# The down projection of a ConvFFN, by seven products of quarters instead of one full product

## The reference, cut to what matters

```
up   = rms_norm(x, g_pre_ffn) @ w_up                # 1024 -> 2 * 2816
conv = b_conv + sum(w_conv[i] * buf[:, i:i + t])    # width 3, causal
hid  = gelu(gate) * val                             # 2816 features
ff   = hid @ w_down                                 # 2816 -> 1024
x    = x + rms_norm(ff, g_post_ffn)
```

## Time and profile before

| | us |
|---|---|
| runs, median (lowest to highest) | 2139.41 (2137.74 to 2140.78) |
| the profiled execution's own time | 2138.59 |
| its span | 2136.8 |
| granted clock of TensorE, mean | 0.994 |
| the 18 Strassen stages, period of each | 21.6 |
| first and last matmul of the down half | 1848.9 and 2127.4 |
| busy in the span: PE, DVE, ACT, POOL | 2070.1, 1419.5, 958.1, 742.8 |

### The profile page before, as it was taken

The page is one execution under the profiler, slowest core; times in us unless marked ns, Lnnn a source line. Parts: engine busy times, 40 slices in busy tenths (PEclk is TensorE's granted clock), DMA queues, the critical chain, the costliest instruction groups (busy, mean ns, idle before and its releaser), DMA issues. The chain is left out here.

```text
span 2136.8 us, 35593 instructions
## 1 busy us (share of the span) xinstructions
PE 2070.1 (97%) x13704; PEld 1953.3 (91%) x13704; DVE 1419.5 (66%) x2242; ACT 958.1 (45%) x1773; POOL 742.8 (35%) x499
## 2 busy tenths in 40 slices
PE   5999999998999999999999999999999999999998
PEld 5998999998899999998999978899999999988875
DVE  5956544443787788857556557598888888834565
ACT  4334534433777777754342122243333333423343
POOL 2333355554644454436565210003333334100000
PEclk9999999999999999999999999999999999999999
DMA  5434344768546555546666433311222222563654
GB/s 175 116 98 133 131 166 166 206 187 238 150 120 144 125 131 142 136 149 176 190 183 205 157 126 99 89 61 61 72 74 79 67 86 62 194 206 127 217 183 163
DMA packets 313278, 298.65 MB, mean 140 GB/s; under 512 B 51767, under 2 KB 275991, under 8 KB 313111
## 3 DMA queue, kind: packets, MB, share of 16 engines
q1 hardware_dynamic: 299776, 265.61, 42.8%
q10 hardware_dynamic: 11094, 22.65, 2.9%
q0 software_dynamic: 2240, 8.13, 1.0%
HBM read 210.03 MB, written 86.30 MB: 139 GB/s over the span
## 5 line engine op out<-in xcount | busy, mean ns | idle before, releaser
L1786 DVE TENSOR_TENSOR_SCAN p_rest<-p_rest 128x896 f32<-128x896 f32 (+7 forms) x128 | 215.0, 1692 | 78.4 <-ACT p_rest L1705 78.4
L1555 POOL TENSOR_TENSOR p_weights<-p_weights,p_rest 128x895 f32<-128x895 f32 (+7 forms) x128 | 162.4, 1275 | 202.6 <-DVE p_rest L1786 202.6
L3355 DVE TENSOR_TENSOR p_w_lo<-p_w_raw,p_w_hi 128x512 fp32r<-128x512 f32 (+1 forms) x168 | 161.0, 963 | 54.4 <-ACT p_w_hi L3147 54.3
L3147 ACT ACTIVATE p_w_hi<-p_w_raw 128x512 fp32r<-128x512 f32 (+1 forms) x186 | 139.3, 772 | 68.0 <-DVE p_rows L3374 37.0
L172 PE MATMUL p_psB<-hT_lo,w_hi 128*128 128x274 f32 (+2 forms) x528 | 161.4, 306 | 4.2 <-issue 2.4
L174 PE MATMUL p_psB<-hT_hi,w_lo 128*128 128x274 f32 (+2 forms) x528 | 159.2, 302 | 0.0
L173 PE MATMUL p_psB<-hT_hi,w_hi 128*128 128x274 f32 (+2 forms) x528 | 159.1, 301 | 0.0
L172 PE MATMUL ps_up<-mergedT_lo,p_w_hi 128*128 128x274 f32 (+1 forms) x488 | 149.2, 306 | 4.1 <-DVE p_rows L3438 1.7
L1130 DVE TENSOR_TENSOR p_x<-p_psB,p_x 128x274 f32<-128x274 f32 (+1 forms) x168 | 70.6, 436 | 118.8 <-PE p_psB L174 113.0
L174 PE MATMUL ps_up<-mergedT_hi,p_w_lo 128*128 128x274 f32 (+1 forms) x488 | 148.4, 304 | 0.0
L173 PE MATMUL ps_up<-mergedT_hi,p_w_hi 128*128 128x274 f32 (+1 forms) x488 | 148.3, 304 | 0.0
(11 more groups left out here) (456 smaller groups left out, 7053.1 us busy)
## 6 DMA issues: line engine op xcount, KB each, us to landing
p_w_raw<-in_w_down SPq DMA_DIRECT2D x66, 512.0 KB, 3.8
p_w_raw<-in_w_up SPq DMA_DIRECT2D x44, 512.0 KB, 5.1
hid_scratch<-p_rows ACTq DMA_DIRECT2D x22, 545.0 KB, 2.9
p_raw_more<-in_w_in SPq DMA_DIRECT2D x20, 512.0 KB, 5.2
w_raw<-in_w_in SPq DMA_DIRECT2D x20, 512.0 KB, 5.3
p_kT<-k_hi_scratch SPq DMA_DIRECT2D x32, 256.0 KB, 4.7
p_kT<-k_lo_scratch SPq DMA_DIRECT2D x32, 256.0 KB, 5.2
w_raw<-in_w_gate SPq DMA_DIRECT2D x16, 512.0 KB, 5.0
```

Of the source, the lines that this page charges most:

```text
L1555: nc.gpsimd.tensor_tensor(wt[:, b % 6, 0:n - 1], wt[:, b % 6, 0:n - 1], rest[:, b % 4, 1:n], ALU.mult).then_inc(s("weights"), 1)
L1786: nc.vector.tensor_tensor_scan(src, src, src, 1.0, ALU.mult, ALU.bypass).then_inc(s("scanned"), 1)
L3147: nc.scalar.activation(target(w_hi, key), source(key), ACT.Copy).then_inc(s("w_hi"), 1)
L3355: nc.vector.tensor_tensor(target(w_lo, key), source(key), target(w_hi, key).bitcast(F32), ALU.subtract).then_inc(s("built"), 1)
```

## The change

The down product gets Strassen's scheme too. The contraction halves are the even and the odd f (11 pairs p, `FP`), the token halves are the lower and upper 512 prompt tokens, the column halves are columns 0 to 511 and 512 to 1023. `DOWN` names the seven products in their order, P1, P2, P5, P6, P3, P7, P4, each over 11 pairs: 77 passes, each of four token tiles with 512 columns, 12 matmuls (924 in all). The 64 sample rows are not part of the scheme: they are multiplied plainly beside P1 and P2 (left half) and P3 and P7 (right half), three matmuls in each of 44 passes (132), as the first of a pass.

The operands are sums: of hidden rows (four sums for each pair, made by POOL during the up half and kept in DRAM in `hid_sums_scratch`) and of quarters of `w_down` (four for each pair, made by POOL in the down half, T1 to T4). The stages in which POOL works on hidden sums are those of `SUMS_OF`: pairs 0 to 2 at f = 6, 7, 8, pairs 3 to 8 at f = 10, 12, 14, 16, 18, 20; pairs 9 and 10 after the last stage. At the start of such a stage POOL issues two loads, at its end it does four additions of 128x512 and issues a store of 1 MB. The products are combined on DVE as they leave PSUM, partly on POOL.

```diff
+    FP = FT // 2
+    DOWN = ("P1", "P2", "P5", "P6", "P3", "P7", "P4")
+    PASSES = [(j, p) for j in range(len(DOWN)) for p in range(FP)]
+    DOWN_BANKS = (4, 5, 6, 7, 1, 2, 3)
+    SUM_AT = {"P6": 0, "P7": 1, "P3": 2, "P5": 3}
+    SUMS_OF = {**{6 + p: p for p in range(3)}, **{2 * p + 4: p for p in range(3, FP - 2)}}
-    BY_TILE = 3
+    BY_TILE = 4
...
@block.gpsimd
+                def bring_hid(p):
+                    pool.wait_ge(s("hid_stored"), 16 * (2 * p + 2))
+                    if p:
+                        pool.wait_ge(s("sums_stored"), 16 * p)
+                    else:
+                        pool.wait_ge(s("t_lo"), 8)
+                    for f in (2 * p, 2 * p + 1):
+                        pool.dma_start(sums[:, 2 * (f % 2):2 * (f % 2) + 2, :].rearrange("p a c -> p (a c)"),
+                                       d.hid[f][:, GAP:GAP + SEQ]).then_inc(s("sums_ready"), 16)
+                def sum_hid(p):
+                    pool.wait_ge(s("sums_ready"), 32 * (p + 1))
+                    for n, (dst, left, right, op) in enumerate(((3, 1, 3, ALU.add), (1, 1, 0, ALU.subtract), (0, 3, 0, ALU.subtract),
+                                                                (2, 2, 0, ALU.subtract))):
+                        if n > 1:
+                            pool.wait_ge(s("hid_sums"), 4 * p + n)
+                        nc.gpsimd.tensor_tensor(sums[:, dst, :], sums[:, left, :], sums[:, right, :], op).then_inc(s("hid_sums"), 1)
+                    pool.wait_ge(s("hid_sums"), 4 * p + 4)
+                    pool.dma_start(d.hs[p], sums[:]).then_inc(s("sums_stored"), 16)
                 for f in range(PLAIN, FT):
                     n, b = 4 * fast(f), 2 * f
+                    if f in SUMS_OF:
+                        bring_hid(SUMS_OF[f])
                     ... (L3016 to L3026)
+                    if f in SUMS_OF:
+                        sum_hid(SUMS_OF[f])
+                for p in (FP - 2, FP - 1):
+                    bring_hid(p)
+                    sum_hid(p)
+                for p in range(FP):
+                    b_sum("T1", p)
+                for p in range(FP):
+                    b_sum("T2", p)
...             (u4 for 4 tiles, T3 for all p, T4 for p < 4, scale_row for 4 tiles of 1024 columns, T4 for the rest,
...              c22_row for 4 tiles, scale_row of the sample, then the right halves of the last four tiles)
@block.tensor
                 def down(i, team):
+                    if team[0] == 0 and name in ("P1", "P2", "P3", "P7"):
+                        last = sample(i, name, p)
+                    for t in team:
+                        if p == 0:
+                            free(j, t)
+                        c = slice(t * P, (t + 1) * P)
+                        last = three_passes(nc, down_bank(j, t), operand_a(a_hi, i)[:, c], operand_a(a_lo, i)[:, c], target(w_hi, key),
+                                            target(w_lo, key), p == 0, p == FP - 1)
@block.sync
+                used(sp, (FT - 1, STEPS.index("A22")))
+                load_sample(0, FT - 1, "sample_most")      # waits for 21 stored hidden tiles; runs of 64 columns
@block.vector, after the last stage
+                weight_lo(("down", 3))
+                sample_lo(0)
+                split_lo(2)
                 convolve(FT - 1, 1)
...
+                for i in range(6, N):
+                    if i % FP == 5 and i > FP:
+                        evict(i // FP - 1)
+                    if i == 68:
+                        normalise(slice(0, TEAM), TEAM)
+                    if 73 <= i < 73 + TEAM:
+                        finish(i - 73)
+                    if i > 6:
+                        split_lo(i - 2)
                     weight_lo(("down", i))
                 for i in (N - 2, N - 1):
                     split_lo(i)
+                normalise(slice(SAMPLE, TILES), TEAM + 1)
+                finish(SAMPLE)
+                evict(DOWN.index("P4"))
+                finish_right(TEAM - 1)
```

More of the change, by code:

```diff
@@ L2816, in earlier @@
     def earlier(key):
-        n = INDEX[key]
-        return OWNER.get(PLACE[n] + SIZE[n] - 1 - OPS)
+        return OWNER.get(PLACE[INDEX[key]] - OPS)
     def fast(f):
         return f - PLAIN
-    def tiles_done(g):
-        return sum(len(TEAMS[x]) for x in range(g + 1))
     def raw_block(key):
-        if key[0] == "down":
-            return 2 * FT + key[1]
         f, j = key
@@ L3094, in down, with sample @@
                         last.then_inc(s("passed"), 1)
-                def free(m):
-                    if m >= 4:
-                        before = max(x for x in range(m) if PAIR[x] == PAIR[m])
-                        pe.wait_ge(s("evac"), before + 1)
-                        if m == 7:
-                            pe.wait_ge(s("tail_rows"), 1)
+                def sample(i, name, p):
+                    key = ("down", i)
+                    n, order = {"P1": (0, 1), "P2": (1, 2), "P3": (0, 4), "P7": (1, 3)}[name]
+                    if p == 0:
+                        pe.wait_ge(s("sample_lo"), order)
+                        if name == "P1":
+                            pe.wait_ge(s("w"), 2 * FAST)
+                        if name == "P3":
+                            pe.wait_ge(s("tail_rows"), 1)
+                    return three_passes(nc, sample_bank(), smp_split[n][:, 0, p, :], smp_split[n][:, 1, p, :], target(w_hi, key),
+                                        target(w_lo, key), p == 0 and name in ("P1", "P3"), p == FP - 1 and name in ("P2", "P7"))
@@ new lines, in _ @@
+                weight_lo(("down", 5))
+                split_lo(4)
+                times(FT - 1)
+                for i in range(6, N):
+                    if i % FP == 5 and i > FP:
+                        evict(i // FP - 1)
+                    if i == 14:
+                        sample_lo(1)
+                    if i == 27:
+                        take_sample(0)
+                    if i == 30:
+                        sample_lo(2)
+                    if i == 31:
+                        sample_sum()
+                    if i == 32:
+                        sample_lo(3)
+                    if i == 68:
+                        normalise(slice(0, TEAM), TEAM)
+                    if i == 71:
+                        take_sample(1)
+                    if 73 <= i < 73 + TEAM:
+                        finish(i - 73)
+                    if i > 6:
@@ L3613, in _ @@
                         split_lo(i - 2)
                     weight_lo(("down", i))
[L3615 to L3618 removed]
+                for i in (N - 2, N - 1):
                     split_lo(i)
[L3620 to L3633 removed]
```

565 lines of the change are left out of this document (357 added, 208 removed).

## The result

The kernel became slower: 2177.95 us, median of four runs (2175.72 to 2179.47), against 2140.1 for the kernel before in the same session (2137.74 to 2141.81), ratio 1.0185, 95% interval 1.0172 to 1.0198 (the ratios here are estimated over all runs of both kernels; the two medians alone give 1.0177). The prediction was 2155, with a range of 2126 to 2170: the direction was right, the size 23 us short, and the time lies 8 us beyond the range.

A forecast was written before the change was run, and what follows sets the result against it. Up half bound by the DVE-ACT loop (21.6 us per stage; PE needs 21.3), down half by PE. 2136.8 - 30.9 + 32.8 + 6.3 + 4 + 4 = 2153.0 span, so 2155 for the median; range 2126 to 2170.

The forecast's parts named there:

- Matmuls: Down half: 1056 matmuls instead of 1188, 132 fewer at 0.234 us, 30.9 us less.
- Hidden sums in the up half: Up-half stages: POOL's additions and loads hold up DVE's convolution, low part and copies; +32.8 us, bounds 5 and 55.
- `c12` in my row: Up-half loop: DVE's `c12`, which reads PSUM and SBUF, was said to keep its 0.39 us.
- Start: Start of the down half: first matmul waits for DVE's `sample_lo(0)`; +6.3 us, bounds 0 and 12.
- my rate: Sample load before the down half: 688 KB at the hidden store's rate, 545 KB in 2.9 us, landing before needed.
- Tail: Last matmul to the end: evictions, row products, root and additions left on DVE; +4 us, bounds 0 and 7.
- I take +4 us of stall, bounds 0 and 12: Late P7: DVE's norm beside POOL's row products takes some 14 us against a lead of three passes, 8.4 to 10.5.
- Rival B: Late down half, P7 and P4: DVE becomes the bound, PE stands some 10 to 15 us, total 2165; chance 0.18.

The follow-up runs named there:

- the run with the stalls gone: Changed kernel with only its late down half reordered (row products, x2 loads, c22 additions, last row work, DVE's norm and row ends): 2164.14 us, ratio 1.0126.

## Why the prediction was wrong, point by point

- *Matmuls*: right. I said 30.9 us less; the run with the stalls gone took 246.9, 31.6 less.
- *Hidden sums in the up half*: near in size, 36.0 for 32.8, and right in mechanism for the larger part. Stages with sums +2.9 (I said 2.85), with loads +1.07 (0.75). The runs without additions, with memsets and with DVE's sums show the cause: POOL's reads of SBUF beside DVE, at a place where the loop has no slack. In detail I had the low part end 2.35 late and the second convolution's copies 0.5 more; the trace has all of it in the first convolution and its low part, 3.1, and the copies are free. For f = 6 and 7, +4.3 for my 3.8, the size was partly luck: I had counted 1.1 us for two loads, and not that POOL must first wait 5.0 us for its own store, which costs nearly as much with memsets in the place of the additions (3.7 and 3.8). And `c12` in my row had no POOL instruction beside it; only the row at 1659.54 above, under L3150, shows that it keeps its 0.39.
- *Start*: right, 7.0 for 6.3. The sample's load took 4.4 us from its issue at 1882.66 and not 3.6, and held ACT for 1.04. The Trainium skill, DMA: Bandwidth & Descriptors, "Specifications", puts line rate at runs of 512 bytes or more. This load has runs of 256 and was slower than my rate, but far from the 7.3 of half that rate; two hidden loads were issued right behind it, so the trace does not show what made the 0.8.
- *Tail*: 5.6 for 4, inside its bounds.
- *"I take +4 us of stall, bounds 0 and 12"*: this step failed. The stall was 23.0, by the run that removed it. The first link was sized rightly (norm 13.4 us, I said 14). I then set it against a lead of three passes on PE's side only. I did not ask who waits for the split queued behind the norm: SP does, at its next hidden load, and behind that load stand the x2 loads and the quarters of `w_down`. So the delay was passed on to the loads, 2 MB went ahead of the needed quarter (8.3 us from issue to landing), and the same order did it again 15 us later. Moved alone, the four row products gave back 7.7 us and the x2 loads 11.5, of which some 3 are the same microseconds. The last gap, 5.5, ends with the split that waited 6.5 us beside POOL's last row work; that row work was moved only together with the rest, so its share is read from the trace and not measured by itself. Rival B saw the place and the lock, and at 10 to 15 us missed the queue as well.

The other rows of the table erred by 2.6 us together (3.2 + 0.7 + 1.6 less the 2.9 ahead of the change); the down half by 18.2, of which the stall is 19.0.

## What to carry to other kernels

Before work is put on an idle POOL, look at what DVE does at that moment, and not at POOL's idle share: 36 additions with their 27 transfers cost 36 us on POOL, and nothing in DVE's own 1.4 us gaps. And an engine that issues a store and then needs the same buffer stands until it has landed, 5 us here, with all its later work behind it. When a step is late, follow it through every queue that waits on it, DMA queues first: a load issuer that waits for compute and then has bulk loads ahead of urgent ones turned a delay of some 14 us at one queue into two rounds of stalls here. And a reordering that frees the bound engine is judged at the tail: here two of three such gains came back there by a third to a half.

## What the hardware showed that I had not expected

- A POOL memset of 1152 columns (1.1 us each) beside DVE's convolution leaves it at 2.75 us for two, where a POOL addition of 512 columns makes it 4.76.
- One DVE instruction can wait for a run of POOL's instructions and not only for the one under way: 6.5 us for the last split, 5.58 for one of a single column, beside instructions of 1.3 to 2.8 us. Why it does not run between two of them is open.
- Width matters for the tiny ones. A tensor_scalar over 4 columns took 2.36 us beside POOL's products of 1024 columns; the same instruction over a single column took 0.15 beside the sample's product (2130.75 in the reordered run, POOL busy from 2130.73 to 2133.13), and only the two tensor_tensor behind it were held up (5.58 and 1.20).
- After the gaps of 2.7, 6.3 and 5.5 us the first matmuls ran at a pitch of 0.425 us for 0.233. The granted clock was 0.50, the lower of its two levels, from 2138.8 to 2141.4, and 0.70 in the mean of 2130 to 2150. In all, the starts from 2104 on lie 24 us further apart than at 0.233, so this is some 2 us beside the 22.0 of the gaps.
